# A sixth quad with seven products in the feed-forward slabs of a decoder layer, with remainders written in place

## The reference

```python
x = x + merged @ w_out[l]
hf = _rms_norm(x, ffn_norm_g[l])
x = x + (jax.nn.silu(hf @ w_ffn_gate[l]) * (hf @ w_ffn_up[l])) @ w_ffn_down[l]
```

## Time and profile before

| | |
|---|---|
| median of 3 runs | 1643.3 us (1643.24 to 1643.5) |
| the profiled execution | 1643.8 us, span of its instructions 1642.0 us |
| TensorE busy | 1634.5 us, 100% of the span |
| VectorE busy | 1141.5 us, 70% |
| ScalarE busy | 874.9 us, 53% |
| moved by DMA | 341.29 MB, mean 208 GB/s |
| granted TensorE clock | 1.00 |

### The profile page before, as it was taken

How to read it: one execution, slowest core, us unless ns; L and a number is a source line. 1 busy time by engine, 2 the same in 40 slices (tenths; PEclk the granted TensorE clock), 3 DMA queues, 4 the chain that set the end, 5 groups by cost and what they waited for, 6 DMA issues and landing times.

```text
span 1642.0 us, 20372 instructions
## 1 busy us (share of the span) xinstructions
PE 1634.5 (100%) x7442; PEld 1352.6 (82%) x7442; DVE 1141.5 (70%) x1161; ACT 874.9 (53%) x954; POOL 79.7 (5%) x73
## 2 busy tenths in 40 slices
PE   9999999999999999999999999999999999999999
PEld 7888888888888888888888888888888888888887
DVE  5565544554577677655555579898898898898894
ACT  6654554444555444444444455656566565565562
POOL 0000000000011100000000000100100100100101
PEclk9999999999999999999999999999999999999999
DMA  9876556566554555566655665877877867968866
GB/s 336 280 207 192 176 156 186 172 192 192 177 167 156 166 167 171 188 230 193 189 186 186 183 208 195 247 252 203 250 242 218 257 233 209 263 227 222 256 226 159
DMA packets 178001, 341.29 MB, mean 208 GB/s; under 512 B 11792, under 2 KB 16400, under 8 KB 177168
## 3 DMA queue, kind: packets, MB, share of 16 engines
q1 hardware_dynamic: 167056, 319.45, 60.6%
q0 software_dynamic: 10880, 20.97, 7.1%
HBM read 317.31 MB, written 2.10 MB: 195 GB/s over the span
## 4 chain that ended last, share of the span: by engine, by line
PE 89%; issue 7%; DVE 2%; DMA 1%; ACT 1%; POOL 0%; SPq 0%; DVEq 0%; ACTq 0%; POOLq 0%
PE acc L1260 47%; PE at L1478 7%; PE at L1477 7%; PE at L1476 7%; PE acc L1476 5%; PE acc L1478 5%; PE acc L1477 5%; PE at L1282 2%; POOL rstd L391 0%; PE at L1335 0%; PE at L1320 0%; DMA raw<-in_w_mem_kv 0%; DVE f_lo L1154 0%; DMA raw<-in_w_in 0%; DVE w_lo L772 0%
## 5 line engine op out<-in xcount | busy, mean ns | idle before, releaser
L772 DVE TENSOR_TENSOR w_lo<-raw,w_hi 128x1024 fp32r<-128x1024 f32 x332 | 402.9, 1224 | 346.3 <-ACT w_hi L418 344.4
L418 ACT ACTIVATE w_hi<-raw 128x1024 fp32r<-128x1024 f32 x332 | 351.5, 1061 | 424.0 <-PE acc L1260 402.8
L1260 PE MATMUL acc<-w_hi,hT_hi 128*128 128x512 f32 x896 | 354.0, 395 | 0.0
L1260 PE MATMUL acc<-w_hi,hT_lo 128*128 128x512 f32 x896 | 349.1, 390 | 0.0
L1260 PE MATMUL acc<-w_lo,hT_hi 128*128 128x512 f32 x896 | 348.9, 389 | 0.0
L1260 PEld LDWEIGHTS acc<-w_hi,hT_hi 128*128 128x128 f32 x896 | 168.2, 188 | 36.4 <-issue 1.3
L1260 PEld LDWEIGHTS acc<-w_hi,hT_lo 128*128 128x128 f32 x896 | 168.2, 188 | 35.6
L1260 PEld LDWEIGHTS acc<-w_lo,hT_hi 128*128 128x128 f32 x896 | 168.3, 188 | 33.9
L1144 DVE TENSOR_TENSOR f_lo<-f_raw,f_hi 128x2048 fp32r<-128x2048 f32 x74 | 168.3, 2285 | 13.3 <-ACT f_hi L696 12.9
L1260 PE MATMUL acc<-w_hi,oT_hi 128*128 128x512 f32 x448 | 176.2, 393 | 1.3 <-DVE oT_lo L791 0.7
L1260 PE MATMUL acc<-w_hi,oT_lo 128*128 128x512 f32 x448 | 174.6, 390 | 0.0
(11 more groups left out here) (213 smaller groups left out, 2091.4 us busy)
## 6 DMA issues: line engine op xcount, KB each, us to landing
raw<-in_w_in SPq DMA_DIRECT2D x208, 512.0 KB, 4.1
f_raw<-in_w_ffn_down SPq DMA_DIRECT2D x88, 512.0 KB, 4.8
f_raw<-in_w_ffn_gate SPq DMA_DIRECT2D x80, 512.0 KB, 4.0
f_raw<-in_w_ffn_up SPq DMA_DIRECT2D x80, 512.0 KB, 5.3
proj<-down POOLq DMA_DIRECT2D x40, 512.0 KB, 8.8
raw<-in_w_mem_kv SPq DMA_DIRECT2D x32, 512.0 KB, 6.3
raw<-in_w_out SPq DMA_DIRECT2D x32, 512.0 KB, 3.7
raw<-in_w_o_mem SPq DMA_DIRECT2D x16, 512.0 KB, 5.0
```

What stands on the lines that cost most here:

```text
L418: act.activation(w_hi[:, s % RING], raw[:, s % RING], ACT.Copy).then_inc(hi_done, 1)
L772: v.tensor_tensor(w_lo[:, s % RING], raw[:, s % RING], w_hi[:, s % RING].bitcast(F32), ALU.subtract).then_inc(lo_done, 1)
L1260: e = pe.matmul(acc[p][:, t, :], a[:, k0 + k, tok], w[:, s % RING, k, :], start=first and k == 0 and n == 0, stop=last and k == 1 and n == 2)
```

## The change

A sixth quad (row blocks 10 and 11) gets seven products, in the place of plain quad N2. `KPAIR` is renumbered, so that the plain quads are N0 and N1. A slab has 18 parts: N0, S0W to S2T, N1, S3W to S5T, D0 to D3. `combine` covers two quads in its second call instead of one.

Remainders of weights are written in place: the remainder of a raw tile over that raw tile, the remainder of a sum over that sum. For this the tiles are allocated, freed and allocated again under fp32r names at the same places. The four `f_lo` tiles go; there are five slots of rounded parts, five raw tiles and three sums. A raw tile is now loaded again when TensorE has finished with its unit, a sum is made again when TensorE has finished its part. `low_three` waits for the sum of its quad, since it overwrites blocks that the sum reads. `u2` lies in `gt[:, 1]`.

D0 now follows S5T directly. It is split by token tile: the first half waits for ACT's copy of `at[:, 0]`, the second for `u2`, and D1 waits for `u_done`. All down chunks run one token tile after the other. ACT's and DVE's orders are otherwise kept.

```diff
-KPAIR = (5, 0, 1, 2, 6, 3, 4, 7)
-UNIT_PART = (0, 1, 3, 5, 7, 8, 10, 12, 13, 14, 15, 16)
-PARTS, UNITS, SLOTS, RAWS, NS = 17, 12, 4, 3, 5
+KPAIR = (6, 0, 1, 2, 7, 3, 4, 5)
+UNIT_PART = (0, 1, 3, 5, 7, 8, 10, 12, 14, 15, 16, 17)
+PARTS, UNITS, SLOTS, RAWS, SUMS, NS = 18, 12, 5, 5, 3, 6
...
+        rest = {name: sb(f"{name}_rest", shape, F32R) for name, shape, dt in layout}
...
+        u2 = gt[:, 1]
...
             def quad(f, u):
-                r = u % RAWS
-                if f > 1 or u >= RAWS:
-                    sp.wait_ge(part_lo, (part(f, UNIT_PART[u - RAWS]) if u >= RAWS else
-                                         part(f - 1, UNIT_PART[u - RAWS])) + 1)
+                g = unit(f, u)
+                r = g % RAWS
+                if g >= RAWS:
+                    sp.wait_ge(part_done, unit_part(g - RAWS) + 1)
...
                 high_three(f, S4W, 6)
                 high_sums(f, S4T, 4)
-                high_whole(f, N2, 7)
+                high_three(f, S5W, 7)
+                high_sums(f, S5T, 5)
                 high_whole(f, D0, 8)
-                act.wait_ge(part_done, part(f, S4W) + 1)
+                act.wait_ge(part_done, part(f, S5W) + 1)
                 act.activation(sg[:, 0], at[:, 0, :], ACT.Copy).then_inc(p1_out, 1)
...
-                    combine(sums[0][:, 0].rearrange("p (k c) -> p k c", c=TOK), last, mixed1, 4, 5, cmb_f4)
+                    combine(sums[0][:, 0:2].rearrange("p q (k c) -> p (q k) c", c=TOK), last, mixed1, 4, 6, cmb_f4)
...
-            def low_three(f, p, u):
+            def low_three(f, p, u, i):
+                v.wait_ge(sum_done, (f - 1) * NS + i + 1)
                 v.wait_ge(part_hi, part(f, p) + 1)
-                v.tensor_tensor(f_lo[slot(f, p)][:, 0:3], f_raw[u % RAWS][:, 1:4], f_hi[slot(f, p)][:, 0:3].bitcast(F32),
+                r = unit(f, u) % RAWS
+                v.tensor_tensor(f_rest[r][:, 1:4], f_raw[r][:, 1:4], f_hi[slot(f, p)][:, 0:3].bitcast(F32),
                                 ALU.subtract).then_inc(part_lo, 1)
...
                 v.wait_ge(p1_out, f)
-                v.wait_ge(part_done, part(f, S4T) + 1)
+                v.wait_ge(part_done, part(f, S5T) + 1)
...
                 sum_rest(f, 4, 6)
-                low_three(f, S4W, 6)
+                sum_first(f, 5, 7)
+                low_three(f, S4W, 6, 4)
                 low_sums(f, S4T, 4)
-                low_whole(f, N2, 7)
+                sum_rest(f, 5, 7)
+                low_three(f, S5W, 7, 5)
+                low_sums(f, S5T, 5)
                 low_whole(f, D0, 8)
                 products_out(f)
                 low_whole(f, D1, 9)
...
-                plain(f, N2, KPAIR[7], False, True)
+                fast_weights(f, S5W, 7, 5)
+                fast_sums(f, S5T, 5)
+                split_ready(f, D0)
+                pe.wait_ge(p1_out, f)
+                down_half(f, D0, 8, 0, 0, aT_hi, aT_lo)
+                pe.wait_ge(u2_made, f)
+                down_half(f, D0, 8, 0, 1, aT_hi, aT_lo).then_inc(part_done, 1)
                 pe.wait_ge(u_done, f)
-                down_chunk(f, D0, 0, aT_hi, aT_lo)
-                down_chunk(f, D1, 1, aT_hi, aT_lo)
+                down_chunk(f, D1, 9, 1, aT_hi, aT_lo)
                 if f == NF - 1:
                     pe.wait_ge(gated_up, f)
                     turn_acts(acc[0])
                 pe.wait_ge(down_out, 4 * f - 3)
```

More of the change, by code:

```diff
@@ L59 @@
 U_KV, U_MQ, U_PROJ, U_MB, U_DB, U_RB, U_OUT, U_F0, U_F = 0, 2, 3, 9, 13, 17, 21, 23, 24
-KPAIR = (5, 0, 1, 2, 6, 3, 4, 7)
-UNIT_PART = (0, 1, 3, 5, 7, 8, 10, 12, 13, 14, 15, 16)
-PARTS, UNITS, SLOTS, RAWS, NS = 17, 12, 4, 3, 5
+KPAIR = (6, 0, 1, 2, 7, 3, 4, 5)
+UNIT_PART = (0, 1, 3, 5, 7, 8, 10, 12, 14, 15, 16, 17)
+PARTS, UNITS, SLOTS, RAWS, SUMS, NS = 18, 12, 5, 5, 3, 6
 ALIGN = 8
-N0, S0W, S0T, S1W, S1T, S2W, S2T, N1, S3W, S3T, S4W, S4T, N2, D0, D1, D2, D3 = range(PARTS)
+SUM_PART = (2, 4, 6, 9, 11, 13)
+N0, S0W, S0T, S1W, S1T, S2W, S2T, N1, S3W, S3T, S4W, S4T, S5W, S5T, D0, D1, D2, D3 = range(PARTS)
 MEM_PIECES = ((0, 2), (2, 4), (4, 8), (8, 12), (12, 16))
@@ new lines, in program @@
+        with ExitStack() as ffn:
+            tile = {name: ffn.enter_context(nc.sbuf_tensor(name, shape, dt)) for name, shape, dt in layout}
+        rest = {name: sb(f"{name}_rest", shape, F32R) for name, shape, dt in layout}
+        aT_hi, aT_lo, down = tile["aT_hi"], tile["aT_lo"], (tile["down0"], tile["down1"])
+        cmb_hi, cmb_lo, cmb_hi4 = tile["cmb_hi"], tile["cmb_lo"], tile["cmb_hi4"]
+        f_hi = [tile[f"f_hi{n}"] for n in range(SLOTS)]
+        f_raw = [tile[f"f_raw{n}"] for n in range(RAWS)]
@@ L175, in program @@
+        f_rest = [rest[f"f_raw{n}"] for n in range(RAWS)]
+        sums = [tile[f"sum{n}"] for n in range(SUMS)]
+        sums_rest = [rest[f"sum{n}"] for n in range(SUMS)]
         sq_flat, qn_flat, pm_flat = (a[:].rearrange(r) for a, r in (
@@ L254, in sum_buf, with unit, unit_part @@
         def sum_buf(f, i):
-            return ((f - 1) * NS + i) % 2
+            return ((f - 1) * NS + i) % SUMS
+        def unit(f, u):
+            return (f - 1) * UNITS + u
+        def unit_part(g):
+            f, u = divmod(g, UNITS)
+            return part(f + 1, UNIT_PART[u])
         def tiles(w, row0, col0):
@@ L350, in _ @@
             for n in range(4):
-                r = n % RAWS
-                sp.wait_ge(part_lo, (part(NF - 1, UNIT_PART[UNITS - RAWS + n]) if n < RAWS else part(NF, 0)) + 1)
+                r = unit(NF, n) % RAWS
+                sp.wait_ge(part_done, unit_part(unit(NF, n) - RAWS) + 1)
                 for k in range(0, 4, 2):
@@ L1166, in sum_rest @@
             def sum_rest(f, i, u):
[L1167 removed]
+                r, t, n = f_raw[unit(f, u) % RAWS], sums[sum_buf(f, i)], (f - 1) * NS + i + 1
                 v.wait_ge(sum_a, n)
@@ L1471, in split_ready, with product, whole, three @@
                 pe.wait_ge(part_lo, part(f, p) + 1)
-            def product(dst, hi, lo, j, b, first, last):
-                whi, wlo = f_hi[j], f_lo[j]
-                pe.matmul(dst, hi, whi[:, b, :], start=first, stop=False)
-                pe.matmul(dst, hi, wlo[:, b, :], start=False, stop=False)
-                return pe.matmul(dst, lo, whi[:, b, :], start=False, stop=last)
+            def product(dst, hi, lo, whi, wlo, first, last):
+                pe.matmul(dst, hi, whi, start=first, stop=False)
+                pe.matmul(dst, hi, wlo, start=False, stop=False)
+                return pe.matmul(dst, lo, whi, start=False, stop=last)
+            def whole(f, p, u, b):
+                return f_hi[slot(f, p)][:, b, :], f_rest[unit(f, u) % RAWS][:, b, :]
+            def three(f, p, u, b):
+                return f_hi[slot(f, p)][:, b, :], f_rest[unit(f, u) % RAWS][:, b + 1, :]
+            def summed(f, p, i, b):
+                return f_hi[slot(f, p)][:, b, :], sums_rest[sum_buf(f, i)][:, b, :]
             def block_a(t, k):
@@ L1483, in combined, with plain @@
             def combined(i, c):
-                return cmb_hi[:, i, c, :] if i < 4 else cmb_hi4[:, c, :], cmb_lo[:, i, c, :]
-            def plain(f, p, q, first, last):
+                return cmb_hi[:, i, c, :] if i < 4 else cmb_hi4[:, i - 4, c, :], cmb_lo[:, i, c, :]
+            def plain(f, p, u, first, last):
                 split_ready(f, p)
@@ L1491, in plain, with plain_half @@
                         for t in range(TB):
-                            e = product(acc[n][:, t, :], *block_a(t, 2 * q + k), slot(f, p), b,
-                                        first and k == 0, last and k == 1)
+                            e = product(acc[n][:, t, :], *block_a(t, 2 * KPAIR[u] + k), *whole(f, p, u, b),
+                                        first and k == 0, last and k == 1 and n == 1 and t == 1)
                 e.then_inc(part_done, 1)
-            def plain_half(n, q):
+            def plain_half(n):
@@ new lines, in fast_sums, with down_half @@
+                product(at[:, 3, :], *combined(i, 3), *summed(f, p, i, 1), i == 0, i == NS - 1)
+                product(at[:, 1, :], *combined(i, 1), *summed(f, p, i, 2), i == 0, i == NS - 1)
+                product(acc[0][:, 1, :], *block_a(1, 2 * i + 1), *summed(f, p, i, 3), False, i == NS - 1).then_inc(part_done, 1)
+            def down_half(f, p, u, n, t, hi, lo):
+                for k in range(4):
+                    e = product(at[:, 2 * (n % 2) + t, :], hi[:, k, t * P:(t + 1) * P],
+                                lo[:, k, t * P:(t + 1) * P], *whole(f, p, u, k), k == 0, k == 3)
+                return e
```

137 lines of the change are left out of this document (62 added, 75 removed).

## The result

| | before | after |
|---|---|---|
| median | 1643.3 us (13 runs, 1642.8 to 1644.3) | 1647.8 us (13 runs, 1644.6 to 1649.7) |
| ratio, 95% interval | | 1.0025 [1.0017, 1.0033] |
| span of the profiled execution | 1642.0 us | 1646.0 us (execution 1647.8) |

The account below looks back on a forecast made before the run. TensorE's matmuls bound the kernel before, with DVE near. Span 1029.4 (slab 1) + 9 x 62.95 + 10.9 + 2.2 + 37.2 = 1646.2 us, 4.2 over before; 1643.3 + 4.2 = 1647.5 us, range 1638.5 to 1653.

Parts of the forecast that it names:

- the likeliest case: DVE and the accumulates' landings set the slab at 62.7 to 63.4 us; 1645 to 1652 us in all; chance 0.45.
- DVE's added work: DVE gains 4.13 us of work a slab, making about 58.7 us of 62.1, so it still fits.
- D2's wait: Each slab, TensorE waits ahead of D2 for ACT's copy of D0, about 0.3 us with the restart.
- The lost cover: N2's 5.44 us of matmuls, between the last sums part and D0, no longer hide products_out and what follows.
- The loop: Accumulates landing in 8.4 or 10.0 us hold copies of D2 and after, delaying low_acts and S5T: 62.95 us a slab.
- the bit that I added for the later of two: Slab end by first or second accumulate, 62.8 or 62.9 us, raised to 62.95 because both scatter.
- (b): Accumulates land under 8 us; TensorE plus the wait at D2 gives 62.4 us a slab, 1642.8 us; chance 0.27.
- The ends: Slab 1's S5T ends at 1029.4, against 1028.2 without a wait; slab 10's transposes lose 2.2 us awaiting the product.
- from D1's end (1604.80) on, 37.2 us remain as they are: The stretch from the last slab's D1 to the end of the span keeps its 37.2 us.
- The sign: The whole kernel gets slower, by 4.2 us; chance 0.47 for slower by over 3.3 us.
- (c): Five slots absorb waits: 1639.9 or 1636.5 us, if low_acts starts before 25.6 and D0's copy ends before 10.6; chance 0.16.
- (d): The two accumulates queue behind one another, the second taking 11.5 us every time: about 1660 us; chance 0.1.

Follow-up runs that it names:

- the rings alone: The changed kernel with its rings and in-place remainders, but N2 a plain quad again and D0 in one piece behind it: 1643.84 us, 1.0003.
- swap on ScalarE's side: The changed kernel with ScalarE rounding the transposed activations ahead of the fourth down copy instead of behind it: 1647.42 us, 1.0024.
- ScalarE's swap on the first run's order: The first run, with ScalarE also rounding the transposed activations ahead of the fourth down copy: 1641.41 us, 0.9983.
- the first run: The changed kernel with DVE's gate and up sums moved ahead of D2's remainder and their product ahead of D3's: 1640.35 us, 0.9982.
- the second experiment: The changed kernel with only the gate and up sums moved ahead of D2's remainder on DVE: 1641.45 us, 0.9991.
- the product alone: The changed kernel with only the product of gate and up moved ahead of D3's remainder on DVE: 1645.06 us, 1.0011.

## Why the prediction was right

**The time and its cause.** Forecast 1647.5, measured 1647.8, and the likeliest case was the one that came. TensorE's saving was taken at 0.68 a slab; the run with the gate sum moved shows 62.79 - 62.13 = 0.66. DVE's added work was right, and so was the zero for writing in place, shown by the rings alone.

**D2's wait.** Put at about 0.3; 0.36 is the difference between the slabs with small accumulates and with the gate sum moved. That the cause is the place of D2's remainder ahead of the gate sum is shown by the latter, where it goes. The lost cover is the right name for it: with N2 back in its place and the order of DVE as in the change (the rings alone), the slabs take 62.79 us, TensorE's own time.

**The loop.** The steps held to 0.1 us. One term was mis-sized: the second accumulate's landing, taken at 10.0 from before, is 8.8. With it the second issue gives 26.4 - 1.2 = 25.2 for low_acts, and only the first one's 26.3 decides; so there was no need for the bit that I added for the later of two, and the slab is 62.83, not 62.95 (though other kernels with the same loop have 62.95 and 62.97). That swap on ScalarE's side in the change, which brought nothing, agrees. That the loop exists is shown by the small accumulates (0.34 a slab), which is its whole price over D2's wait; forecast 62.95 - 62.4 = 0.55. The sizes of the landings were taken over from before and not worked out: the first one's 8.4 held because the load is issued just ahead of it, as the prediction said under (b), and it is 5.9 where that is not so.

**The rule of the Trainium skill.** By the Trainium skill, page DMA: Bandwidth & Descriptors, section on the anatomy of one DMA, 512 KB would take an estimated 3.2 us and 64 KB an estimated 2.2. The traces do not agree: no accumulate of the change lands under 5.1 us, and the small ones landed in 2.7 to 6.7. With 3.2 us no copy would be held and the slab would take 62.4. The small-accumulate run shows what the slab is when almost none is held: 62.49, close to the 62.4 of the second rival.

**The ends.** Slab 1 lost 62.14 - (60.98 - 0.66) = 1.8 us, D2's 0.36 among it; forecast 1.2 + 0.3. It started 0.7 us earlier than in the profile of before, which hid that in the sum. (That start lies between 988.7 and 990.4 from kernel to kernel. The latest, ScalarE's swap on the first run's order, has a granted clock of 0.89 and 0.54 from 6 to 9 and 9 to 12 us; the others were not looked into.) The last turn's 2.2 us measured 2.0.

**What the sum did not have.** The step "from D1's end (1604.80) on, 37.2 us remain as they are" failed: 39.05. Of the 1.85 us, 1.7 are matmuls at the lower clock after the idle of 2.0; two kernels that have the idle and not the low clock take 37.4. Against that stand slabs 2 to 10, 1.7 us under the forecast, and the early start. Errors of both signs make the total agree better than its parts, and that it came within 0.3 us is luck. The sign does not rest on the clock. A low stretch of 1.7 us is 0.001 of the span, so it lowers the mean granted clock of a timed run to 0.999 or less. Five of the 13 runs of the change read 1.000: their times are 1644.6 to 1647.9, median 1646.95, which is 3.6 over before and above all 13 runs of before. The other eight have a median of 1647.9.

**The rivals.** (b), accumulates under 8 us, did not come for the copies of D0 and D1, whose landings decide. (c), faster, comes with the edit that its condition names: with the gate sum moved, the copy of D0 ends before D2 wants it, and the time is 1641.45. It is 1.5 over the 1639.9 reckoned for clean slabs with both ends lost. The slots alone did not absorb the waits; the order had to change. (d), 11.5 for every second accumulate, did not come (10.3 at most).

## What to carry to other kernels

When an edit takes work off the engine that bounds the kernel, ask what that work was hiding: here 5.4 us of matmuls covered a chain over DVE, ScalarE and a DMA that cost TensorE nothing before. Follow the new chain instruction by instruction before the change is made; moving one pair of adds ahead of a remainder that nobody was waiting for gave back 6.4 us of the change's time, and left 2 us of gain over the kernel before. Before an instruction is moved forward, look at what lets go the load it reads, not only at what stands around it.

## What was not expected of the hardware

**The clock.** In the kernel after, the idle of 2.0 us ahead of the last transposes is followed by a granted clock of 0.62 and 0.53. The windows of the second experiment, with the same idle of 2.0:

```profile
1600.00:1602.00 2.00, 0.33 (x3) 0.33 (x4) 2.00 (x3) 0.97 (x2) 0.73 (x1) 1.00 1.13 171
1602.00:1604.00 2.00, 2.00 (x14) 1.74 (x12) 1.82 (x1) 1.20 (x2) 0.47 (x1) 1.00 0.96 208
```

The clock stays at 1.00. Of five profiled kernels with that idle, three show the longer end (the change 39.05 us from the last turn, small accumulates 39.0, the product alone 39.1), two do not (37.4 in both: the gate sum moved, and the change with ScalarE's swap). So the length of the idle time alone does not decide; what does is open. It makes such a wait cost either 2.2 or 3.9 us. Nor do all timed runs pay: with the idle of 2.0, 20 of the 51 runs of these five kernels have a mean granted clock of 1.000, without it 50 of the 70 runs of the other seven edited kernels. A reading under 1.000 does not say where in the run the clock was low: the product alone also has 0.50 from 9 to 12 us, and other profiles have some at the very end, when TensorE is done.

**Accumulates.** A DMA of 512 KB that adds to its target took 5.1 to 10.3 us to land among the loads, and one of 64 KB still 2.7 to 6.7: an eighth of the bytes took about half of the time (medians 4.0 and 8.3). Where an accumulate stands among the loads moves it by about as much: the first of a pair takes 8.4 us on average behind a load issued 0.3 us ahead of it, and 5.9 when it is issued 1.9 us ahead of the load; of the small ones, the first takes 5.1 to 6.7 behind the load and the second, 3 us later, 2.8 to 3.9. How much of the landing is the adding itself was not measured, and no run moves a load alone.
